# Weight loads of a decoder step: two chunks per transfer of 1 MB instead of one chunk per 512 KB

## What is computed

```
h    = rmsnorm(x, g_pre)
proj = einsum('btd,dn->btn', h, w_in)        # n: q k v o za | ig fg | u vb zb ga gb, 2048 columns each (ig, fg: 8)
q, k = silu(causal_conv4([q_pre, k_pre]))    # 8 heads of 256
hn   = rmsnorm_per_head(mlstm(q, k, v, ig, logsigmoid(fg), C0, n0, m0))
y_a  = sigmoid(o) * hn * silu(za)
y_b  = u * (tril(w_s[g]) @ layernorm(vb) + b_s[g]) * silu(zb)
out  = (sigmoid(ga) * (y_a @ w_pa) + sigmoid(gb) * (y_b @ w_pb)) @ w_out
y    = x + rmsnorm(out, g_post)
```

## Time and profile before

| | |
|---|---|
| median of 3 runs | 1455.55 us (1455.39 to 1456.16) |
| the profiled execution | 1456.57 us, of which the span of the trace is 1455.1 us |
| TensorE busy | 1443.6 us, 99% of the span |
| VectorE, ScalarE, GpSimd busy | 60%, 43%, 15% |
| TensorE's granted clock | the upper of its two levels, 2.4 GHz, in all 40 slices |
| DMA engines | about 59% busy with the hardware queue and 10% with the software queue |

### The profile page before, as it was taken

How to read it: one execution, slowest core, us unless ns; L and a number is a source line. 1 busy time by engine, 2 the same in 40 slices (tenths; PEclk the granted TensorE clock), 3 DMA queues, 4 the chain that set the end, 5 groups by cost and what they waited for, 6 DMA issues and landing times.

```text
span 1455.1 us, 31107 instructions
## 1 busy us (share of the span) xinstructions
PE 1443.6 (99%) x11067; PEld 1421.4 (98%) x11067; DVE 877.5 (60%) x1481; ACT 626.0 (43%) x887; POOL 217.6 (15%) x362
## 2 busy tenths in 40 slices
PE   9999999999999999999999999999999999999998
PEld 8999999999999999999999999999999999999997
DVE  7877565564444347676767677676767554544444
ACT  6444433333333334444445454535454433333442
POOL 4142000001000000404141413131312000000000
PEclk9999999999999999999999999999999999999999
DMA  8585655557655568596969696979797665565554
GB/s 247 148 229 143 185 149 172 164 149 240 190 173 175 179 187 216 161 305 171 302 178 294 180 295 173 298 179 293 188 287 176 205 183 172 175 181 177 190 163 160
DMA packets 311573, 292.13 MB, mean 201 GB/s; under 512 B 82960, under 2 KB 297560, under 8 KB 310896
## 3 DMA queue, kind: packets, MB, share of 16 engines
q1 hardware_dynamic: 292368, 242.99, 58.8%
q0 software_dynamic: 19088, 48.58, 10.1%
q10 hardware_dynamic: 80, 0.07, 0.0%
HBM read 266.12 MB, written 25.44 MB: 200 GB/s over the span
## 4 chain that ended last, share of the span: by engine, by line
PE 96%; DMA 2%; DVE 1%; ACT 0%; issue 0%; SPq 0%; POOL 0%; DVEq 0%; ACTq 0%; POOLq 0%
PE ps L461 29%; PE ps L462 29%; PE ps L460 29%; DMA raw<-in_w_in_dram 1%; PE ps L647 1%; PE ps L730 1%; PE ps L683 1%; DMA xt<-in_x_prompt_dram 1%; PE ps L616 1%; PE ps L658 0%; DVE wlo L1093 0%; PE ps L740 0%; PE ps L496 0%; PE ps L691 0%; PE ps L711 0%
## 5 line engine op out<-in xcount | busy, mean ns | idle before, releaser
L1093 DVE TENSOR_TENSOR wlo<-raw,whi 128x1024 fp32r<-128x1024 f32 x416 | 507.6, 1224 | 500.3 <-ACT whi L832 498.3
L832 ACT ACTIVATE whi<-raw 128x1024 fp32r<-128x1024 f32 x416 | 439.3, 1058 | 665.1 <-PE ps L462 630.2
L460 PE MATMUL ps<-xh,whi 128*128 128x288 f32 x2304 | 683.2, 297 | 0.0
L461 PE MATMUL ps<-xl,whi 128*128 128x288 f32 x2304 | 682.0, 296 | 0.0
L462 PE MATMUL ps<-xh,wlo 128*128 128x288 f32 x2304 | 679.0, 295 | 0.0
L460 PEld LDWEIGHTS ps<-xh,whi 128*128 128x128 f32 x2304 | 433.6, 188 | 4.8 <-issue 2.5
L461 PEld LDWEIGHTS ps<-xl,whi 128*128 128x128 f32 x2304 | 433.1, 188 | 0.4
L462 PEld LDWEIGHTS ps<-xh,wlo 128*128 128x128 f32 x2304 | 432.9, 188 | 0.0
L460 PE MATMUL ps<-yh,whi 128*128 128x288 f32 x768 | 227.5, 296 | 0.6 <-DVE yl L1112 0.6
L461 PE MATMUL ps<-yl,whi 128*128 128x288 f32 x768 | 227.3, 296 | 0.0
L462 PE MATMUL ps<-yh,wlo 128*128 128x288 f32 x768 | 226.4, 295 | 0.0
(11 more groups left out here) (357 smaller groups left out, 1079.3 us busy)
## 6 DMA issues: line engine op xcount, KB each, us to landing
raw<-in_w_in_dram SPq DMA_DIRECT2D x320, 512.0 KB, 3.9
raw<-in_w_pb_dram SPq DMA_DIRECT2D x32, 512.0 KB, 3.5
Cin<-in_state_mlstm_C_dram POOLq DMA_DIRECT2D x16, 1024.0 KB, 8.4
Xb<-in_state_mlstm_C_dram SPq DMA_DIRECT2D x256, 64.0 KB, 3.8
out_dram<-Cin POOLq DMA_DIRECT2D x16, 1024.0 KB, 6.0
raw<-in_w_pa_dram SPq DMA_DIRECT2D x32, 512.0 KB, 3.5
raw<-in_w_out_dram SPq DMA_DIRECT2D x32, 512.0 KB, 3.5
bcs<-rows_d POOLq DMA_DIRECT2D x8, 304.0 KB, 3.6
```

What stands on the lines that cost most here:

```text
L460: nc.tensor.matmul(out, whi[:, c, kk, cols], mh_[:, k, :], start=(k == 0), stop=False)
L461: nc.tensor.matmul(out, whi[:, c, kk, cols], ml_[:, k, :], start=False, stop=False)
L832: nc.scalar.activation(whi[:, c], raw[:, c], ACT.Copy).then_inc(hi_ready, 1)
L1093: nc.vector.tensor_tensor(wlo[:, c], raw[:, c], whi[:, c].bitcast(F32), ALU.subtract).then_inc(lo_ready, 1)
```

## The change

From the second pair on, SyncE asks for chunks 0 and 1 of a pair by one transfer of 1 MB, and for chunks 2 and 3 by another. It waits until VectorE has read both buffers of the two. The landing raises `raw_landed[0]` or `raw_landed[2]` alone, and ScalarE waits for a landing ahead of chunks 0 and 2 only. The first pair is loaded as before. The rows in DRAM are still cut into runs of 1 KB (256 columns), so that the two descriptions name the same bytes.

```diff
-    def chunked(w):
-        return w.rearrange("(c k p) n -> c p k n", k=CK, p=P)
+    def chunked(w, k):
+        return w.rearrange("(c k p) n -> c p k n", k=k, p=P)
 
-    w_in_v, w_pa_v, w_pb_v, w_out_v = (chunked(w) for w in (w_in, w_pa, w_pb, w_out))
+    w_in_v, w_pa_v, w_pb_v, w_out_v = (chunked(w, 2 * CK) for w in (w_in, w_pa, w_pb, w_out))
+    w_first = chunked(w_in, CK)
...
         def load_pair(pair, w, col, first=False, blocks=None):
             for c in range(CHUNKS):
-                if not first:
-
-                    sp.wait_ge(lo_ready, 4 * pair - 3 + c)
+                if first:
+                    sp.dma_start(raw[:, c], w[c, :, :, ds(col, PW)]).then_inc(raw_landed[c], 16)
...
+                elif c % 2 == 0:
+                    sp.wait_ge(lo_ready, 4 * pair - 2 + c)
                     sp.nop(nofuse=True)
-                sp.dma_start(raw[:, c], w[c, :, :, ds(col, PW)]).then_inc(raw_landed[c], 16)
...
+                    sp.dma_start(raw[:, c:c + 2].rearrange("p c k n -> p (c k) n"),
+                                 w[c // 2, :, :, ds(col, PW)]).then_inc(raw_landed[c], 16)
...
-        load_pair(V0, w_in_v, COL_VB, first=True)
+        load_pair(V0, w_first, COL_VB, first=True)
...
-            act.wait_ge(raw_landed[c], 16 * pair + 16)
+            if first or c % 2 == 0:
+                act.wait_ge(raw_landed[c], 16 * pair + 16)
```

More of the change, by code:

```diff
@@ L387, in load_pair @@
             for c in range(CHUNKS):
-                if not first:
-                    sp.wait_ge(lo_ready, 4 * pair - 3 + c)
-                    sp.nop(nofuse=True)
-                sp.dma_start(raw[:, c], w[c, :, :, ds(col, PW)]).then_inc(raw_landed[c], 16)
[L393 to L396, removed]
+                if first:
+                    sp.dma_start(raw[:, c], w[c, :, :, ds(col, PW)]).then_inc(raw_landed[c], 16)
+                    if c == 1:
+                        sp.dma_start(xt[0:S, 2, D // 4:], xs_v[:, D // 4:]).then_inc(x_in[1], 16)
+                    sp.dma_start(xt[:, 0:2, QUARTERS[c]], xp_v[:, :, QUARTERS[c]]).then_inc(x_in[c], 16)
+                elif c % 2 == 0:
+                    sp.wait_ge(lo_ready, 4 * pair - 2 + c)
+                    sp.nop(nofuse=True)
+                    sp.dma_start(raw[:, c:c + 2].rearrange("p c k n -> p (c k) n"),
+                                 w[c // 2, :, :, ds(col, PW)]).then_inc(raw_landed[c], 16)
                 if blocks is not None:
```

## The result

| | median | runs |
|---|---|---|
| before | 1455.86 us | 1455.39 to 1456.76 |
| with joint loads | 1482.59 us | 1480.64 to 1483.74 |

What follows compares the result with a forecast made beforehand. TensorE, busy 1443.6 of 1455.1 us, was taken to bound the kernel. Steady stretches 0, jam +5.4 and heads 0 us on 1455.55 gave 1461.0 us, own range 1459.0 to 1463.5, with the first rival 1455.9 to 1463.6.

Steps and rivals of the forecast that it cites:

- the cover in the heads: Chunk 188 in the second head: whi waits for chunk 189, TensorE keeps 2.6 us of cover; costed at 0 us.
- the half-delivered transfer in the jam: Chunks 20 and 21, 71 to 92 us: about half still queued at the jam, landing at 91.5 us; net +5.4 us.
- The third rival: Heads: joint transfer beside state loads over 2.6 us late makes TensorE wait in some six heads; 1464 to 1469 us, chance 0.05.
- The jam: Stretch at 71 to 92 us where loads are held: TensorE waits 6.7 us for chunk 20, net +5.4 us.
- my first rival: Jam: chunks 20 and 21 land by 84.8 us, only 22 and 23 late by 1.3 us; 1456.8 us, chance 0.32.
- the wait at the transposes: TensorE's 1.3 us of idleness before the transposes at L551, forecast to vanish.
- The first rival's worst case: Jam: joint transfer of chunks 20 and 21 landing at 89.2 us, said to leave about 2.9 us.
- the chances of the forecast and of the heads: Chances 0.60 for the forecast and 0.05 for the heads losing cover, given as 0.64 for slower by over 0.2%.
- Steady stretches: Outside jam and heads: 1 MB lands in 5.8 us (bounds 3.9 and 7.8), TensorE's 7.2 us cover it; 0 us.

Runs made afterwards that it cites:

- e4: Changed kernel with TensorE's product with the Yb columns moved one chunk later, after the fourth chunk of the v pair: 1464.81 us, ratio 1.0053.
- e2: Kernel before, transfers and requests unchanged; only ScalarE, ahead of an even chunk, waits until the odd one has landed too: 1478.96 us, ratio 1.0162.
- e3: Changed kernel with the v pair of each head loaded by four 512 KB transfers as before, everything else joint: 1463.32 us, ratio 1.0047.
- e8: Changed kernel with GpSimd loading the next head's states (Cin) only after VectorE has read the v pair's chunks: 1461.29 us, ratio 1.0034.
- e11: Changed kernel with broadcasts spread, Yb product one chunk later and Cin loads later: 1454.77 us, ratio 0.9991.
- e6: Changed kernel with broadcasts spread and TensorE's Yb product one chunk later: 1457.28 us, ratio 1.0008.
- e12: Kernel before with the scattered m_s store moved to the end of GpSimd's transfers, gmn in its own place: 1455.06 us, ratio 0.9997.
- e9: Kernel before without the scattered m_s store (output unwritten), broadcasts where they were: 1454.81 us, ratio 0.9991.
- e7: Kernel before (512 KB loads) with GpSimd's three broadcasts issued later and apart: 1454.92 us, ratio 0.9993.
- e10: Kernel before without the m_s store and with the three broadcasts spread: 1454.82 us, ratio 0.9993.

## Why the prediction was wrong

**Direction right, size wrong by a factor of five.** I forecast 1461.0 us, 5.4 us slower, with a range to 1463.6; it is 27 us slower. Three steps failed: the cover in the heads, the half-delivered transfer in the jam, and the clock.

*The heads ("Cover left: 2.6 us ... I cost it at nothing").* This is the failure that counts: 21.5 of the 25.3 us between the two profiles. I saw that `whi` of chunk 188 would wait for chunk 189 and that it would be 3.7 us late; it was 4.8. I then measured the cover at the consumer of the chunk itself, TensorE's first matmul on it. The next thing in VectorE's order that TensorE needs is not that chunk but the `Yb` columns, 15 us further down, which were ready 0.8 us ahead of TensorE. VectorE had only 1.2 us of idle time between `wlo` 188 and the columns, so 3.6 of the 4.8 us of lateness arrive there. At the transposes I had followed ScalarE's order behind the late chunk to the copy that TensorE wants; in the heads I did not follow VectorE's. e4 moves only that consumer and the loss goes; e2 makes only the even chunk wait for the odd and the loss comes.

*The third rival ("the heads lose their cover")* named the place, at a chance of 0.05, but its price went by the same cover: it wanted a landing 2.6 us later than the order of the queue gives, where none was needed.

*The jam ("about half of it ... is still queued when the jam begins").* Wrong in how much was left. I gave the joint transfer the rate that chunk 21 had had, but 512 KB had taken 5.1 us there because only 512 KB were asked for. From the request to 76 us SyncE's queue moved 0.97 MB, against 0.52 MB before, and GpSimd's 0.18 MB against 0.35:

```profile
q1 hardware_dynamic: 954, 0.97, 77.2%
q0 software_dynamic: 132, 0.18, 11.0%
```

So under a tenth was left, not half. This rest came through while all engines together moved 97 GB/s, and the transfer landed at 83.9, before the 84.8 that my first rival set as the limit. Chunk 20 was in time, and chunk 22 was late by the 1.25 us that this rival gives. That I took the nearest row, chunk 22's, for a transfer which entered the queue 3.5 us earlier was the error. The rival's total, +1.3 us, was still too small, and that the landing stayed under its limit was partly luck: in e3, e4 and e8 the same transfer landed at 84.9 to 87.0 us, and TensorE did wait for chunk 20, though for 0.9 to 1.95 us and not for 6.7. Nor did the wait at the transposes vanish there: it was 2.9 to 3.0 us.

*The clock*, which no term of mine had. The rival's 1.3 us became 4.0, since behind the longer wait TensorE ran at 1.2 GHz; with three of the heads it makes 7.8 us of longer matmuls, a third of the loss. The profile before could not show a price, but it showed the full clock in all slices, beside waits of at most 1.8 us. I should have asked what a longer one does.

*Two sums.* The first rival's worst case, 89.2 + 2.4 - 87.2 - 1.3, is 3.1 us and not 2.9; the chances of the forecast and of the heads add up to 0.65, not 0.64. Neither changes the forecast.

*What held.* Steady stretches cost nothing, and 1 MB lands in 5.2 us, near my 5.8 and between the bounds. No joint load outside the two places costs anything (e11, and the profile of e6). TensorE had no idle time that larger transfers could have given back. The Trainium skill's advice in "DMA: Bandwidth & Descriptors", section "Bandwidth", to batch to 1 MiB, holds for the rate: 1 MB in 5.2 us against 512 KB in 3.9. TensorE waited for no load's rate; what was lost is that the consumer of the first half could have begun before the second had landed.

## What to carry to other kernels

Joining two transfers joins their landings: the first half's consumer waits for the second half's bytes, and that is dear exactly where something else shares the DMA engines. When a producer gets later, follow each in-order engine past the item itself to the next thing on it that the bounding engine wants, and measure the cover there. Price a wait of the bounding engine with what its clock does behind it, not with the wait alone.

## What the runs showed of the hardware

**A tiny scattered store held the DMA engines.** Storing 64 values of 4 bytes took 10.4 us in the kernel before (its landing ended ScalarE's wait of 6.9 us there) and 7.5 us in e12. Beside the broadcasts the engines moved 29 GB/s from 76 to 82 us with it and 406 without it (e9); without the broadcasts 87 with it (e7) and 153 without (e10). In e12 they moved 108 GB/s from 1320 to 1326 us, against 174 to 194 in the 30 us before. A 512 KB load behind it took 9.3 us at 74 us (e7), where it took 3.7 without the store (e10), and 9.1 us at 1321 us (e12). The sister store of 8 values, issued just before it, landed in 1.6 us, and with it alone (e10) no load was held. A transfer that was nearly through was caught as well: of the 1 MB that the changed kernel requested at 70.65, just before the store at 70.71, 0.97 MB had moved by 76 us, and it landed at 83.9. The Trainium skill, "DMA: Bandwidth & Descriptors", section "Specifications", says that below 512 B the DMA engines do read-modify-write; that would fit, but the runs show only the store's effect, not its mechanism.

**The clock.** After idle stretches of 2.85 and 2.88 us TensorE's granted clock fell to 0.5, for 6.8 and 3.4 us; in e2 it also fell in two heads whose waits were 2.2 us each. But in e3 it stayed at 1.0 behind a wait of 3.0 us at the transposes, and in the changed kernel behind one of 2.2 us in the seventh head. So the length of the wait alone does not tell whether the clock falls; what else decides, these runs do not show.
